# A two-layer backbone kernel on Trainium2: adds and maxima of the attention dealt anew, inputs of most stages loaded a stage ahead, one block of a projection left out, the output stage reordered

## The reference

```python
for layer in range(DEPTH):                      # DEPTH = 2
    h = rms_norm(x, norm_g[layer]) * (1.0 + scale) + shift      # both streams; shift, scale, gate from SiLU(c)
    if layer % 2 == 0:
        y_lat, y_ctx = even_mixer(h_lat, h_ctx, ...)   # 8-head attention beside Fourier mixing, gate, w_out
    else:
        y_lat, y_ctx = odd_mixer(h_lat, h_ctx, ...)    # RWKV-7 in both directions, gate, w_out; y_ctx not needed
    x = x + gate * y_lat
```

## Time and profile before

| | |
|---|---|
| median of 3 runs | 5268.63 us (5265.32 to 5269.36) |
| the profiled execution | 5257.98 us; span in the trace 5256.2 us |
| mean granted TensorE clock | 0.966 of full speed |
| PE busy | 4710.6 us, 90% of the span |
| DVE, ACT, POOL busy | 50%, 35%, 25% |
| DMA | 526.39 MB, 100 GB/s on average |

### The profile page before, as it was taken

The page is one execution under the profiler, slowest core; times in us unless marked ns, Lnnn a source line. Parts: engine busy times, 40 slices in busy tenths (PEclk is TensorE's granted clock), DMA queues, the critical chain, the costliest instruction groups (busy, mean ns, idle before and its releaser), DMA issues. The chain is left out here.

```text
span 5256.2 us, 121695 instructions
## 1 busy us (share of the span) xinstructions
PE 4710.6 (90%) x49854; PEld 2635.2 (50%) x49854; DVE 2605.3 (50%) x4105; ACT 1816.4 (35%) x4359; POOL 1297.3 (25%) x2820
## 2 busy tenths in 40 slices
PE   6999997999999998999999999967878888888689
PEld 3666663333333333454444444436666666666544
DVE  2444444667666661231222222245666666666476
ACT  1221212433434330231212111135556656555322
POOL 0111111222222220000000000005555565565333
PEclk8999997999999998999999999988999999999899
DMA  5222221000000007331111211135666666666485
GB/s 203 93 85 89 86 75 53 23 23 11 17 23 22 24 21 287 139 136 51 60 60 65 67 60 60 56 93 137 148 151 141 152 145 147 150 152 149 111 271 169
DMA packets 925174, 526.39 MB, mean 100 GB/s; under 512 B 658581, under 2 KB 876309, under 8 KB 916632
## 3 DMA queue, kind: packets, MB, share of 16 engines
q1 hardware_dynamic: 843482, 496.91, 32.8%
q10 hardware_dynamic: 81216, 22.73, 2.1%
HBM read 331.00 MB, written 188.49 MB: 99 GB/s over the span
## 5 line engine op out<-in xcount | busy, mean ns | idle before, releaser
L1611 PE MATMUL p_bU<-keep_hT,p_slab 128*128 128x512 f32 (+1 forms) x2592 | 1029.9, 559 | 12.5 <-DMA p_slab<-in_o_w_in_dram 7.0
L1611 PEld LDWEIGHTS p_bU<-keep_hT,p_slab 128*128 128x128 f32 x2592 | 493.6, 191 | 543.7 <-issue 512.3
L924 PE MATMUL at_bS<-at_qT,at_kT 97*64 97x512 f32 (+1 forms) x2368 | 611.3, 602 | 4.0 <-ACT at_pT L1022 2.3
L1059 DVE TENSOR_REDUCE at_mx<-at_bM 128x1 f32<-128x512 f32 (+1 forms) x656 | 391.0, 627 | 268.6 <-PE at_bM L889 265.2
L1022 ACT ACTIVATE at_pT<-at_bS 128x512 f32<-128x512 f32 (+1 forms) x592 | 339.9, 591 | 429.8 <-PE at_bS L924 360.4
L1683 DVE SCALAR_TENSOR_TENSOR p_z<-p_u,p_shift,p_z 128x2306 f32<-128x2306 f32 x26 | 68.2, 2621 | 770.2 <-ACT p_z L1641 770.2
L1938 POOL TENSOR_TENSOR rw_g_at<-rw_g_at,rw_g_prod 64x14 f32<-64x14 f32 (+6 forms) x1008 | 314.4, 312 | 79.0
L1936 POOL TENSOR_TENSOR rw_g_prod<-rw_g_at 64x14 f32<-64x14 f32 (+6 forms) x1008 | 311.8, 309 | 79.1
L1080 DVE TENSOR_TENSOR at_sum_vector<-at_sum_vector,at_pT 128x512 f32<-128x512 f32 x320 | 300.8, 940 | 43.6 <-ACT at_pT L1022 28.2
L2395 DVE TENSOR_TENSOR rw_S<-rw_bank,rw_dec 128x128 f32<-128x128 f32 x288 | 84.1, 292 | 452.2 <-PE rw_bank L2116 452.2
L943 PE MATMUL at_bO<-at_pT,at_va 128*64 128x512 f32 x1152 | 301.9, 602 | 0.0
(11 more groups left out here) (270 smaller groups left out, 9499.8 us busy)
## 6 DMA issues: line engine op xcount, KB each, us to landing
rw_zin<-scratch_heads SPq DMA_DIRECT2D x144, 512.0 KB
rw_XB<-scratch_inverses SPq DMA_DIRECT2D x576, 64.0 KB
scratch_heads<-p_z SPq DMA_DIRECT2D x24, 1024.0 KB, 4.9
rw_lin<-scratch_lora SPq DMA_DIRECT2D x144, 128.0 KB
scratch_bv<-rw_bv SPq DMA_DIRECT2D x144, 128.0 KB
scratch_products<-rw_NB SPq DMA_DIRECT2D x288, 64.0 KB
scratch_y<-rw_ysb ACTq DMA_DIRECT2D x288, 64.0 KB, 2.7
p_slab<-in_o_w_in_dram SPq DMA_DIRECT2D x34, 512.0 KB, 5.8
```

The costliest lines, as they stand in the source:

```text
L924: last = pe.matmul(bS[rows, g % 3, 0:nq * P], kT[:, s, k * P + VH * x:k * P + VH * x + VH], qT[:, s, q0 * P:(q0 + nq) * P], start=True, st ...
L1059: nc.vector.tensor_reduce(mx[:, j, piece:piece + 1], bM[:, (FIRST_ITEM[b] + i) % 2, 0:n], AX.X, ALU.max).then_inc(max_red, 1)
L1611: last = pe.matmul(bU[:, n % 4, 0:w], slab[:, i, k, :], hT[:, k, tok:tok + w], start=(k == 0), stop=(k == KD - 1))
```

## The change

- **modulate, project0.** `ident`, `bias` and `norm_g` are issued by ACT's queue. SiLU waits for the two conditioning vectors only, DVE for `ident` and for the columns. modulate's semaphores are cleared by SP in project0. PE waits for `prep` before the q matmuls of each tile. Some buffers of project0 move into a new kept tile, `wide` (4 MB), which later stages use in turn.
- **attend.** `on_pool` takes odd pairs (1, 3, 5, 7; pair 8 stays on DVE) instead of every third (1, 4, 7). The maxima of the next block start at step 1 and end at step 14 (two at a step in which POOL adds) instead of 0 to 12, and the row follows at step 15 instead of 14; ACT's copy of the row stands at the same place. SP loads fourier's `step1` and the first half of `ab` (`ab0`) at the stage's start.
- **fourier.** Only the second half of `ab` and the context's inputs are loaded in the stage. After the `zin` loads SP waits for step 1's matmuls and loads merge0's weights into `wide`, ahead of the stores of `fo`. **merge0** has no weight loads.
- **project1.** Receptance leaves the context block out too (`FIRST`), and ACT and DVE skip those columns. SP clears the earlier stages' semaphores early in the stage, and before the last pair loads rwkv's first inputs and constants.
- **rwkv.** No loads at its start; PE waits for the constants only at the first bonus. At the end SP loads merge1's first gates and `x` tiles and the 4 MB of `o_w_out`.
- **merge1.** `y` of tile 0 is loaded first. POOL sums bonus 0 before its two `rstd`; ACT evicts tile 0 before it squares tile 1; DVE merges tile 0 after centring tile 1. In the loop DVE runs centre, normalise, merge, scale, residual (before: centre, merge, normalise, scale, residual). PE's first tile is written out: half a product, the turn of tile 1, the other half.

The diff, cut to its core:

```diff
-                    sp.dma_start(bias[:], A["ada_b"][0].rearrange("(m p) -> p m", p=P)).then_inc(small, 16)
-                    for layer in range(2):
-                        sp.dma_start(norm_g[:, layer, :], A["norm_g"][layer].rearrange("(k p) -> p k", p=P)).then_inc(small, 16)
-                sp.dma_start(keep["ident"][:], A["ident"]).then_inc(small, 16)
...
-                a.wait_ge(small, 6 * 16)
+                a.dma_start(keep["ident"][:], A["ident"]).then_inc(tables, 16)
+                with nc.allow_non_contiguous_dma("short vectors as columns"):
+                    a.dma_start(bias[:], A["ada_b"][0].rearrange("(m p) -> p m", p=P)).then_inc(columns, 16)
+                    for layer in range(2):
+                        a.dma_start(norm_g[:, layer, :], A["norm_g"][layer].rearrange("(k p) -> p k", p=P)).then_inc(columns, 16)
+                a.wait_ge(small, 2 * 16)
...
+                v.wait_ge(tables, 16)
                 nc.vector.tensor_reduce(pick[:], keep["ident"][:].rearrange("p (g s) -> p s g", g=GROUPS)[:, 0:2, :], AX.X, ALU.add).then_inc(set_up, 1)
+                v.wait_ge(columns, 3 * 16)
...
+                for one in opened:
+                    sp.sem_clear(one)
...
+                    pe.wait_ge(prep, 2)
...
-                pe.wait_ge(prep, 2)
...
-            return STEPS[b] > 2 and pair % 3 == 1
+            return STEPS[b] > 2 and pair % 2 == 1
...
-                full, rows = (h, s, b + 1), [(nk - 4, h, s, b + 1)]
+                full, rows = (h, s, b + 1), [(nk - 3, h, s, b + 1)]
...
-                    rows.append((nk - 4, h + 1, 1 - s, 0))
+                    rows.append((nk - 3, h + 1, 1 - s, 0))
             if full:
                 i = 0
-                for k in range(nk - 5):
-                    for _ in range(2 if k < 3 or on_pool(b, (k - 2) // 2) else 1):
+                for k in range(1, nk - 3):
+                    for _ in range(2 if k > 1 and on_pool(b, (k - 2) // 2) else 1):
...
+                sp.dma_start(fourier_tables(keep), A["step1"]).then_inc(keep["ab_l"][0], 16)
+                sp.dma_start(keep["ab0"][:], W["fx"][CTX:T].rearrange("(p n) c -> p n c", n=N2)[:, 0:N2 // 2]).then_inc(keep["ab_l"][0], 16)
...
-                            for kind, hh, ss, bb, i in jobs[k - 2] if k > 1 else ():
+                            for kind, hh, ss, bb, i in jobs[k - 1] if k else ():
...
-                sp.dma_start(step1[:, 0:CH], A["step1"][:, 0:CH]).then_inc(tab, 16)
-                sp.dma_start(ab[:, 0:CH], src[:, 0:CH]).then_inc(ab_l[0], 16)
-                sp.dma_start(step1[:, CH:N2], A["step1"][:, CH:N2]).then_inc(tab, 16)
-                for i in range(1, N2 // CH):
-                    sp.dma_start(ab[:, CH * i:CH * (i + 1)], src[:, CH * i:CH * (i + 1)]).then_inc(ab_l[i], 16)
+                sp.dma_start(ab[1][:], src[:, HN:N2]).then_inc(ab_l[1], 16)
...
+                sp.wait_ge(mm1, N2)
+                for j in range(2):
+                    cols = slice(j * 512, (j + 1) * 512)
+                    sp.dma_start(keep["wide"][:, :, cols], A["e_w_out"][0, :, cols].rearrange("(k p) n -> p k n", p=P)).then_inc(keep["m0_w_l"][j], 16)
...
-                for j in range(2):
-                    cols = slice(j * 512, (j + 1) * 512)
-                    sp.dma_start(w[:, :, cols], A["e_w_out"][0, :, cols].rearrange("(k p) n -> p k n", p=P)).then_inc(w_l[j], 16)
...
+        FIRST = (0, 0, 1, 1)
+        AT = [sum(NB - f for f in FIRST[:i]) for i in range(5)]
+        PB = AT[4]
...
+                for one in finished:
+                    sp.sem_clear(one)
...
+                sp.wait_ge(z_st[0], 32 * 3)
+                sp.wait_ge(z_st[1], 32 * 2)
+                sp.wait_ge(kk_st, 32)
...
+                        sp.dma_start(zin[:, n, d], W["heads"][0, :, :, first:first + GT]).then_inc(keep["rw_in_l"][n], 16)
+                        sp.dma_start(lin[side, n], W["lora"][:, side, first:first + GT].rearrange("i c t -> c i t")).then_inc(keep["rw_in_l"][n], 16)
...
+                for name in ("reset", "same", "tri", "far"):
+                    sp.dma_start(keep["rw_" + name][:], A[name]).then_inc(keep["rw_c_l"], 16)
...
+                        blocks(i, base, AT[i], FIRST[i])
...
+                    if m.n == 0:
+                        pe.wait_ge(c_l, 16 * 10)
...
+                for s in range(2):
+                    sp.dma_start(keep["m1_gs"][:, s], W["gsT"][:, :, s * P:(s + 1) * P].rearrange("k p t -> p k t")).then_inc(keep["m1_b_l"][s], 16)
+                    sp.dma_start(keep["m1_xt"][:, s], W["x1"][CTX + s * P:CTX + (s + 1) * P, :]).then_inc(keep["m1_x_l"][s], 16)
+                sp.wait_ge(tr_mm[2], NBODY)
+                sp.wait_ge(ar_done, 2 * NBODY)
+                sp.wait_ge(kb_done, NBODY)
                 sp.wait_ge(bv_st, 32 * NBODY)
+                sp.dma_start(keep["wide"][:], A["o_w_out"][0].rearrange("(k p) n -> p k n", p=P)).then_inc(keep["m1_w_l"], 16)
...
+                load_y(0, 0)
                 with nc.allow_non_contiguous_dma("short vectors as columns"):
                     for i, name in enumerate(("o_gn_w", "o_gn_b")):
                         sp.dma_start(gn[:, i, :], A[name][0].rearrange("(k p) -> p k", p=P)).then_inc(c_l, 16)
-                for t in range(2):
-                    load_y(t, t)
-                    load_bonus(t, t)
-                sp.dma_start(w[:], A["o_w_out"][0].rearrange("(k p) n -> p k n", p=P)).then_inc(w_l, 16)
-                for t in range(2):
-                    load_x(t, t)
+                load_bonus(0, 0, False)
+                load_y(1, 1)
+                load_bonus(1, 1, False)
...
                 g.wait_ge(half_set, 1)
+                bonus(0, 0)
                 rstd(0)
                 rstd(1)
-                bonus(0, 0)
...
                 turn(0, 0)
                 pe.wait_ge(w_l, 16)
-                iterations(pe.Fori, one)
+                pe.wait_ge(o_done, 1)
+                pe.wait_ge(y_free, 1)
+                project(0, 0)
+                turn(1, 1)
+                project(0, 1)
+                one(1, 1, True, True)
+                iterations(pe.Fori, one, 1)
...
                 square(0)
-                square(1)
                 a.wait_ge(c_l, 32)
                 evict(0)
+                square(1)
...
                     centre(t, t, link)
+                    if t == 1:
+                        merge(0, 0)
                     normalise(t, t, link)
                     scale(t, t)
-                merge(0, 0)
 
                 def one(t, s, next1, next2):
                     link = Link(v, dch, ML * (t + 2))
                     if next2:
                         centre(t + 2, s, link)
+                        normalise(t + 2, s, link)
                     if next1:
                         merge(t + 1, 1 - s)
                     if next2:
-                        normalise(t + 2, s, link)
                         scale(t + 2, s)
                     residual(t, s)
...
+            finished = list(used)
+            project1(nc, sem, keep, A, W, finished)
+        clear_semaphores(nc, used[len(finished):])
```

204 lines of the change are left out of this document (109 added, 95 removed).

## The result

The changed kernel takes 5173.46 us (median of 4 runs, 5170.87 to 5174.95), the kernel before 5267.99 (4 runs, 5265.32 to 5269.36). The ratio is 0.982, 95% interval 0.9805 to 0.9836: faster by 94.5 us. Forecast were 5174 and a range of 5135 to 5215. The profiled executions lie closer together: 5170.87 against 5257.98, 87.1 us by either the runs or the spans, 5169.1 against 5256.2. The sum of the prediction was made against the profiled execution, where it says -94.8; so 7.7 us of the fine match in the medians is luck, and the parts have to be looked at one by one.

What follows compares the result with a forecast made beforehand. TensorE was taken to bound attend and project1, something else the joints between stages and merge1. The terms summed to -94.8 us: 5163.2 from the profiled 5257.98, 5174 applied to the median 5268.63; range 5135 to 5215.

Steps and rivals of the forecast that it cites:

- A, start: Start through project0: earlier first matmul, -2.5 us, and the wait for scaled w_uq moved to the q matmuls, -3.1; together -5.6.
- B, attend: attend: new order of adds, maxima and row shortens TensorE's waits for DVE; -16 us, bounds -50 to +20.
- the row's new wait: attend: the row one step after the last maximum costs 0.3 us in each of 32 blocks, +10.
- at_o's wait: attend: row transposes' 20.1 us wait for DVE's at_o shrinks, -12 us; the sign was falling below 10 us.
- the maxima: attend: the four maxima together at step 0 of the last block become two, -6 us.
- the half clock: attend: half of the clock losses behind the row waits, 3 us up to seven times, go; -8 us.
- load is moved, hardly taken away: attend: DVE's busy time changes by only -16 us of 753, though it loses 64 adds to POOL.
- Rival 4: attend: POOL's four pairs a block block DVE's adds on the path; +111 us in full, 5301 us total, chance 0.04.
- C, fourier and merge0: fourier and merge0: earlier loads -8.8 us, output stores delayed behind merge0's weights +12, merge0's first transposes -10; together -7.
- D, project1: project1: receptance's context block goes, 128 of 416 matmuls fewer; -27.4 us, bounds -28 and -20.
- E: Step from project1 to rwkv: moved semaphore clears -8.1 us and earlier loads -12.9; together -21.
- F, merge1: merge1: first matmul 9 us earlier, then TensorE bounds the loop, -0.7 us x 13 tiles = -9; together -18.

Runs made afterwards that it cites:

- e7: Changed kernel with layer 1's norm_g waited for in fourier instead of modulate; project0's first transposes at 55.2 us instead of 59.8.
- e4: Kernel before with POOL's attend adds over 64 of 512 columns; attend 1098.0 us against 1125.6.
- e11: Changed kernel with POOL's attend adds over 64 of 512 columns and PE's old first-tile order in merge1; attend 1105.2 us (1104.8), merge1 250.4 (250.8).
- e6: Changed kernel with merge0's weights issued by ACT's queue instead of SP's; fourier 120.1 us against 122.2.
- e8: Changed kernel with merge1's old DVE loop order and receptance's context block back; project1 1079.0 us (1051.5), merge1 256.5 (250.8).
- e10: Changed kernel with merge1's first gate product ahead of merge and attend's step 13 extra maximum at step 3; merge1 246.0 us (250.8), attend 1100.3 (1104.8).

## Why the prediction was right, and where it was not

- **A, start, -5.6: -4.0.** The gain of silu was there (2.8 us at the first matmul for 2.5), and so was the moved wait; the late norm_g, which the prediction did not have, held modulate's last step back to 48.3 us, and e7 shows what that cost: 4.5 us at project0's first matmul. The prediction had put the small loads on another queue and called them early, but the engines behind both queues were full.
- **B, attend, -16: -20.8.** Near in sum, and wrong in one of its reasons. Right: the row's new wait (+10 forecast, 14.5 - 2.3 = 12 for ACT), at_o's wait (-12; it is -8.4, and 11.7 us are left where "below 10" was the sign), the maxima (-6; -11.4), the half clock (-8; -10.4). Wrong: "load is moved, hardly taken away". DVE's adds lost 106 us: 64 adds at 0.94 us, and 0.18 us of each of the other 256; "the means of L1080 rise" had the wrong sign. Rival 4, the hold-up by POOL, was there in before (27.6 us, e4) and left hardly more than 3 us in after (e11): the change was the way out of it, not into it.
- **C, fourier and merge0, -7: -7.3.** Up to step 2 -9.8 for -8.8, step 2 +12.1 for +12, merge0 -9.6 for -10. Right in every size. The last was booked to the wrong tile: the 10.92 us of the earlier trace rows are the second tile's, and the first transposes wait 9.5 us as before, not 1. The mechanism behind +12 was full engines more than the order in the queue (e6).
- **D, project1, -27.4: -27.8** (e8: 27.5).
- **E, -21: -21.4.** The two parts, the clears and the loads, were not taken apart by any run.
- **F, merge1, -18: -7.3. The step that failed.** "-9" at the start: the first product is 8.0 us earlier, but the chain on DVE and POOL to the third turn decides, and all edits of the start are worth 1.6 us (e8 against before), PE's split nothing (e11). "TensorE bounds: -0.7 x 13": it did not; the chain takes 14.9 us, POOL's power being 0.9 longer behind merge's product, and 5.7 us is what the order is worth (e8). Only e10 has the period of 14.6 that was forecast.

The sum by these stretches is -88.7 us, and rwkv (+1.2) and the borders (+0.4) make it -87.1. That it comes near -94.8 is partly luck: attend gave 4.8 us more than forecast, merge1 10.7 less. The medians are 94.5 apart, because the profiled execution of before lay 10.0 below its median and that of after 2.6. rwkv's stretch, 1460.0 to 1477.8 us with the same code, is large enough for that; which stretch it was in the timed runs no profile tells.
